# Splitting the weight transfers of the last four expert pairs, not the last two, in a decoder-layer kernel

## The chip, the core and the metric

The kernel runs on one core of a Trainium2 chip. The time is the device time of one execution in microseconds. All arithmetic is in 32-bit floats.

## What is computed

One layer of a decoder for 256 prompt tokens and 64 sample tokens (320 in all, 1024 features): a modulated norm, a mixer (gated MLP heads and a state-space part) with a gated residual, then a modulated norm and a mixture of 32 experts of which each token takes four, a gated residual and a last norm. The mixture is what this text is about:

```
logits = x @ w_router + b_router
top_v, top_i = top_k(logits, 4);  top_w = softmax(top_v)
for each expert e, on the rows of the tokens that chose it:
    g = minimum(xb @ w_gate[e] + b_gate[e], 7.0)
    u = clip(xb @ w_up[e] + b_up[e], -7.0, 7.0)
    y = (g * sigmoid(1.702 * g) * (u + 1.0)) @ w_down[e] + b_down[e]
out[token] = sum over its 4 experts of top_w * y
```

Each of the three matrices of an expert is 1024 x 1024, so an expert has 12.6 MB of weights and all of them 403 MB. Each is used once.

## The kernel before

The first 260 us or so are the mixer and the router (weights `w_front`). Then the experts are worked off in 16 **pairs**, 0 to 15. A pair's two experts share the 128 columns of the TensorE array, 64 token rows for each (`CAP`), or 96 and 32 in pairs 2 to 5. The gathered rows are the stationary operand and the weights stream past them.

*Transfers.* A pair's weights come in 12 transfers (`PER`), numbered k = 0 to 11, of 2 MB each: k even is for the first expert of the pair and k odd for the second, and each brings four chunks (`CHUNKS`) of 128 input features times 1024 outputs of one matrix. So k = 0 to 3 are `w_gate`, 4 to 7 `w_up`, 8 to 11 `w_down`. They land in a ring of 8 slots (`RING`), 16 MB of on-chip memory; `SLOT` says which slot each takes. In the text the fourth transfer of a pair is k = 3, the eighth is k = 7, and so on.

*SyncE* issues all of them in program order (the functions at L566 to L587). Ahead of each it waits for the semaphore `exp_used`, which TensorE raises when it has finished with the slot that the transfer overwrites. The transfer's landing raises `exp_landed` of its slot by 16.

*TensorE.* `pair` (L1010) does the three products gate, up and down of a pair, and between them the gathering of the next pair's rows, the turning of the activations and the combining of the pair before. A `product` (L962) is two bias matmuls and then two halves, p = 0 and 1, of 32 matmuls each; half p needs two transfers, one for each expert. It waits for both `exp_landed` at its start (L976). ScalarE and VectorE take the results from PSUM when `exp_used` says that the product is done.

*Split transfers.* `FS` is 6, so `SPLIT` = 12 - 6 = 6. In the last two pairs, 14 and 15, the transfers k = 6 to 11 are each issued as two of 1 MB, two chunks each, by `load_split` (L522), in the order: first half of k, first half of k + 1, second half of k, second half of k + 1. The first half raises the slot's `exp_landed`, the second one a semaphore left over from the front part (`split_landed`, L477). In these pairs the product waits in two steps: for the two first halves at its start, and for the two second halves ahead of its third chunk (L984 to L986). `split_count` (L480) gives the count to wait for. SyncE waits once for both slots of k and k + 1 before it issues the four halves.

*Loops.* Two pairs are a **turn** (`UNROLL`). All engines run the turns through `turns` (L212): turns 0, 1 and 2 (pairs 0 to 5) are written out, turns 3 to 6 (pairs 6 to 13) are one loop in the program, whose addresses and counts come from registers, and turn 7 (pairs 14 and 15) is written out. SyncE has a loop of its own (L575) over turns 1 to 6. Pair 15 goes through `last_pair` (L1048), which has another order of the small steps: it combines pair 14 between gate and up, and lets the down product begin on the first half of the activations. Behind it come the output additions, the last norm and the stores.

Of the kernel before, what the change touches and what calls it, by code (L numbers as in the profile page):

```python
# [65 lines left out]
FS = 6  # L66
# [5 lines left out]
UNROLL = 2  # L72
PAIRS = NE // 2
LAST = PAIRS - 1
SPLIT = PER - FS
MORE_PAIRS = -(-MORE // 2)
LW = 2 * MORE_PAIRS


def caps(q):  # L80

    return (WIDE, NARROW) if isinstance(q, int) and q in UNEVEN else (CAP, CAP)
# [90 lines left out]
NF = len(FRONT)  # L173
# [32 lines left out]
def wait(eng, sem, count):  # L206

    if not (isinstance(count, int) and count <= 0):
        eng.wait_ge(sem, count)


def turns(engine_loop, body):  # L212

    even = max(UNEVEN) // UNROLL + 1
    for i in range(even):
        body(i)
    with engine_loop(even, PAIRS // UNROLL - 1) as i:
        body(i)
    body(PAIRS // UNROLL - 1)


def further_pairs(engine, there, begin, body, again):


    with engine.If(there(engine, 0) == 1):
        begin()
        body(0)
        with engine.If(there(engine, 1) == 1):
            with engine.Fori(1, MORE_PAIRS) as i:
                with engine.If(there(engine, i) == 1):  # L230
# [4 lines left out]
def build(nc, d, out):  # L235
    with ExitStack() as ctx:
# [240 lines left out]
        def split_landed(k):  # L477
            return front_landed[k - SPLIT]

        def split_count(q, k):  # L480
            return 16 * (len(range(k - SPLIT, NF, FS)) + q - (PAIRS - UNROLL) + 1)

        def exp_slot(j, k):
            return SLOT[(PER * j + k) % RING]
# [13 lines left out]
        def chosen(eng, q):  # L498

            return [eng.value_load(expert_i[0:1, bass.ds(q * 2 + s, 1)], min_val=0, max_val=NE - 1) for s in range(2)]  # L500
# [5 lines left out]
        def _(sp):  # L506
# [9 lines left out]
            def load_unit(k, e, slot):  # L516
                sp.dma_start(ring[:, slot, :], exp_source(k, e)).then_inc(exp_landed[slot], 16)  # L517
# [4 lines left out]
            def load_split(k, e, slots):  # L522

                w = [exp_source(k + s, e) for s in range(2)]
                for part in range(2):
                    c = slice(part * LOAD // 2, (part + 1) * LOAD // 2)
                    for s in range(2):
                        done = exp_landed[slots[s]] if part == 0 else split_landed(k + s)
                        sp.dma_start(ring[:, slots[s], c], w[s][:, c]).then_inc(done, 16)
# [38 lines left out]
            def sorted_pair(i, j):  # L568
                es = chosen(sp, i * UNROLL + j)
                for k in range(PER):  # L570
                    sp.wait_ge(exp_used, i * (PER * UNROLL) + (PER * j + k - RING + 1))
                    load_unit(k, lambda s: es[s], exp_slot(j, k))

            sorted_pair(0, 1)
            with sp.Fori(1, PAIRS // UNROLL - 1) as i:  # L575
                for j in range(UNROLL):
                    sorted_pair(i, j)
            for j in range(UNROLL):
                q = PAIRS - UNROLL + j
                es = chosen(sp, q)  # L580
                for k in range(PER):
                    if k < SPLIT:
                        sp.wait_ge(exp_used, q * PER + k - RING + 1)
                        load_unit(k, lambda s: es[s], exp_slot(j, k))
                    elif k % 2 == 0:
                        sp.wait_ge(exp_used, q * PER + k + 1 - RING + 1)
                        load_split(k, lambda s: es[s], [exp_slot(j, k + s) for s in range(2)])  # L587
# [30 lines left out]
        def _(pe):  # L618
# [262 lines left out]
            for m in range(KC):  # L881
# [5 lines left out]
                for i in range(KC):  # L887
                    k = (i + 4) % KC
# [55 lines left out]
            def gather(q):  # L944

                wait(pe, sel_ready, q + 1)
                wait(pe, selT_ready, q - 1)
                for k in range(KC):
                    for t in range(NT):
                        last = mm(ps[:, 6 + k // 4, (k % 4) * P:(k % 4 + 1) * P], htok[:, t, k * P:(k + 1) * P],  # L950
                                  moe["sel"][:, t, :], t == 0, t == NT - 1)
                    if isinstance(q, int) and q == 0 and k == KC // 2 - 1:
                        last.then_inc(half_mm, 1)
                last.then_inc(x_mm, 1)

            def turn_act():

                for k in range(KC):
                    last = pe.transpose(ps[:, k // 4, (k % 4) * P:(k % 4 + 1) * P], A[:, k, :], cn("ident"))  # L959
                last.then_inc(a_tr, 1)  # L960

            def product(m, bank, rows, loads, slots, widths=(CAP, CAP), between=None, half_done=None, mid=None, q=None):  # L962
# [9 lines left out]
                for p in range(KC // CHUNKS):  # L972
# [8 lines left out]
                    for at, (kk, half) in enumerate(order):  # L981
                        if mid is not None and (p, kk, half) == (0, CHUNKS - 2, 0):
                            mid()
                        if q is not None and at == CHUNKS and m * PER // 3 + 2 * p >= SPLIT:  # L984
                            for s in range(2):
# [9 lines left out]
            def combine(q):  # L995

                pe.wait_ge(y_ready, q + 1)
                pe.wait_ge(selT_ready, q + 1)
                for m in range(KC):
                    wait(pe, comb_added, q * KC + max(0, m - 2))  # L1000
                    mm(ps[:, (2, 3, 6)[m % 3], 0:T], moe["y"][:, m * P:(m + 1) * P], moe["selT"]).then_inc(comb_mm, 1)

            def turn_sel(q):

                pe.wait_ge(selw_ready, q + 1)
                for t, (t0, r) in enumerate(TILES):
                    last = pe.transpose(ps[:, 7, t0:t0 + r], moe["selw"][0:r, t, :], cn("ident", r, r))  # L1007
                last.then_inc(selT_tr, 1)

            def pair(q, slots, loads, serial=False):  # L1010
                first = isinstance(q, int) and q == 0
                if serial:
                    wait(pe, comb_added, q * KC)
                    gather(q)
                if first:
                    pe.wait_ge(half_copied, 1)
                else:
                    pe.wait_ge(x_ready, q + 1)
                pe.wait_ge(pick_ready, q + 1)
                w = (CAP, CAP) if serial else caps(q)  # L1020
                split = isinstance(q, int) and PAIRS - UNROLL <= q < PAIRS
                product(0, 0, X, loads[0:PER // 3], slots[0:PER // 3], w, (lambda: pe.wait_ge(x_ready, 1)) if first else None)
                if first:
                    turn_table()
                if not first:
                    wait(pe, comb_added, (q - (0 if serial else 1)) * KC)
                if isinstance(q, int) and q == 2:
                    pe.wait_ge(more_read, 1)
                product(1, 2, X, loads[PER // 3:2 * PER // 3], slots[PER // 3:2 * PER // 3], w, sort_table if first else None,
                        q=q if split else None)  # L1030
                if not serial:
                    gather(q + 1)
                pe.wait_ge(act_ready, q + 1)
                turn_act()
                if not serial:
                    pe.wait_ge(x_ready, q + 2)
                if not serial and not first:
                    combine(q - 1)
                turn_sel(q)
                pe.wait_ge(actT_ready, q + 1)  # L1040
                wait(pe, y_ready, q)
                later_middle = None
                if isinstance(q, int) and q == 1:
                    later_middle = further_blocks
                product(2, 4, A, loads[2 * PER // 3:PER], slots[2 * PER // 3:PER], w, later_middle,
                        q=q if split else None)
# [48 lines left out]
            def turn_table():  # L1095

                pe.wait_ge(perm_ready, 1)
                mm(ps[:, 5, P:P + NE], cn("eidx", NE), perm[0:NE, :])
                mm(ps[0:NE, 5, 0:1], perm[0:NE, :], count[0:NE, :])
                pe.wait_ge(table_ready, 1)  # L1100
                for t, (t0, n) in enumerate(TILES):
                    last = pe.transpose(ps[0:2 * NE, 4, t0:t0 + n], table[0:n, :, t], cn("ident", n, n))
                last.then_inc(tableT_mm, 1)
# [26 lines left out]
            def pe_turn(i):  # L1130
                for j in range(UNROLL):
# [4 lines left out]
                    else:  # L1136
                        pair(i * UNROLL + j, slots, loads)

            turns(pe.Fori, pe_turn)
            final_sums(0)  # L1140
            pe.wait_ge(more_ready, 1)
# [12 lines left out]
        def _(act):  # L1154
# [204 lines left out]
            def last_copies():  # L1359
# [11 lines left out]
                A(moe["y"][:, AW:D], ps[:, 5, :], ACT.Copy).then_inc(y_ready, 1)  # L1371

            turns(act.Fori, act_turn)

            def squares(r):
# [23 lines left out]
        def _(dve):  # L1399
# [492 lines left out]
            def dve_turn(i):  # L1892
                nonlocal start
                for j in range(UNROLL):
# [29 lines left out]
                    if second:  # L1924
                        start = start + 2

            turns(dve.Fori, dve_turn)
            add_last()
            final_norm(0)
# [168 lines left out]
```

## Time and profile before

| | us |
|---|---|
| median of three runs | 1196.75 |
| lowest, highest of them | 1194.54, 1199.53 |
| the profiled execution, its own time | 1195.16 |
| its span, first to last instruction | 1193.2 |
| TensorE busy, matmuls | 1144.8 (96%) |
| VectorE busy | 293.9 (25%) |
| ScalarE busy | 153.4 (13%) |
| expert weights moved by SyncE's queue | 180 transfers of 2 MB, 24 of 1 MB |
| mean granted TensorE clock, share of full | 0.985 |

Times in the profile count from the first instruction of the span. The share of TensorE in its own span says little here, since a loop in which TensorE and the DMA engines are nearly equally fast shows both as busy. What is wanted is who waits for whom, pair by pair, and which wait is the last one that the end depends on. The line L620 is the helper through which every matmul goes, L517 issues a whole transfer and L529 a half.

### The profile page before, as it was taken

What the parts mean: (1) busy time and instruction counts of PE and PEld (TensorE: products, weight loads), DVE (VectorE), ACT (ScalarE), POOL (GpSimd) and SP (SyncE); (2) the same over time, 40 slices, a digit from 0 to 9 for tenths busy, and PEclk for the clock granted to TensorE, in tenths of its full rate; (3) what the DMA queues carried; (4) which work ended last, traced back from release to release, by engine and by line L of the source; (5) the groups of instructions that cost most, each with busy time, mean ns of one, the idle gap of its engine ahead of it and who ended that gap; (6) DMA issues with size and microseconds to landing.
All of it is one profiled execution on the core that took longest, in us unless ns stands there. A gap on an engine that the chain in (4) does not pass through costs nothing.

```text
span 1193.2 us, 15523 instructions
## 1 busy us (share of the span) xinstructions
PE 1144.8 (96%) x6471; PEld 532.9 (45%) x6472; DVE 293.9 (25%) x667; ACT 153.4 (13%) x258; POOL 32.1 (3%) x46
## 2 busy tenths in 40 slices
PE   5999999999999999999999999999999999999995
PEld 2666556554353524243535353434343444434332
DVE  3254422422121213030303031212121212121143
ACT  1442141311000000000101010101010101011002
POOL 1030201000000000000000000000000000000000
PEclk9899999999999999999999999999999999999998
DMA  9574567649999999999999999999999999999992
GB/s 381 226 272 156 221 272 313 263 183 429 417 428 422 428 422 427 426 427 427 425 428 428 427 426 429 429 430 426 429 429 430 427 428 429 430 427 420 429 419 90
DMA packets 38788, 452.67 MB, mean 379 GB/s; under 512 B 4176, under 2 KB 6608, under 8 KB 7632
## 3 DMA queue, kind: packets, MB, share of 16 engines
q1 hardware_dynamic: 37984, 449.31, 89.8%
q0 software_dynamic: 752, 2.60, 0.6%
q8 instruction: 40, 0.66, 0.2%
q14 instruction: 12, 0.10, 0.0%
HBM read 447.99 MB, written 3.91 MB: 379 GB/s over the span
## 4 chain that ended last, share of the span: by engine, by line
PE 76%; DMA 19%; ACT 2%; DVE 1%; issue 1%; SPq 0%; DVEq 0%
PE ps L620 75%; DMA arena<-in_w_exp 18%; ACT arena L1320 1%; DMA arena<-in_w_front 1%; DVE arena L1404 1%; DMA arena<-in_xT 1%; PE ps L1007 0%; SPq L517 0%; PE ps L776 0%; DVE arena L1810 0%; DVE arena L1808 0%; DVE arena L1789 0%; ACT arena L1180 0%; PE ps L797 0%; PE ps L1065 0%
## 5 line engine op out<-in xcount | busy, mean ns | idle before, releaser
L620 PE MATMUL ps<-arena 128*64 128x512 f32 (+10 forms) x6226 | 1115.5, 519 | 37.5 <-DMA arena<-in_w_exp 14.3
L620 PEld LDWEIGHTS ps<-arena 128*64 128x64 f32 (+4 forms) x6226 | 505.4, 147 | 638.4 <-issue 568.4
L1320 ACT ACTIVATE arena<-ps 128x1024 f32<-128x1024 f32 x45 | 44.4, 1021 | 516.4 <-PE ps L620 516.4
L1746 DVE TENSOR_SCALAR arena<-ps 128x1024 f32<-128x1024 f32 x15 | 18.3, 1223 | 266.0 <-PE ps L620 266.0
L1404 DVE TENSOR_TENSOR arena<-arena 128x1024 f32<-128x1024 f32 (+11 forms) x91 | 66.2, 749 | 53.1 <-ACT arena L1328 16.8
L1404 DVE TENSOR_TENSOR arena<-arena,ps 128x320 f32<-128x320 f32 (+2 forms) x116 | 57.0, 494 | 69.2 <-PE ps L620 64.2
L1754 DVE TENSOR_SCALAR arena<-ps 128x1024 f32<-128x1024 f32 x15 | 18.4, 1224 | 183.6 <-PE ps L620 183.6
L1328 ACT ACTIVATE arena<-arena 128x1024 f32<-128x1024 f32 x16 | 16.9, 1057 | 243.8 <-DVE arena L1746 228.3
L1739 DVE COPY arena<-arena 128x64 f32 (+3 forms) x32 | 5.0, 193 | 124.9 <-PE ps L620 124.9
L1404 DVE TENSOR_TENSOR arena<-ps,arena 128x64 f32<-128x64 f32 (+10 forms) x39 | 13.2, 354 | 40.1 <-PE ps L620 35.3
L1732 DVE TENSOR_SCALAR arena<-arena 128x64 f32<-128x64 f32 (+3 forms) x96 | 23.0, 302 | 0.1
L1462 DVE SCALAR_TENSOR_TENSOR arena<-arena 128x344 f32<-128x344 f32 x24 | 13.7, 576 | 26.0 <-ACT arena L1211 25.3
L1755 DVE SCALAR_TENSOR_TENSOR arena<-arena 128x1024 f32<-128x1024 f32 x15 | 18.4, 1225 | 0.5
L1725 DVE TENSOR_SCALAR arena<-arena 128x64 f32<-128x64 f32 (+3 forms) x96 | 17.0, 246 | 1.9 <-issue 1.5
L959 PE MATMUL ps<-arena 128*128 128x128 f32 x120 | 15.6, 272 | 0.0
L1336 ACT ACTIVATE arena<-ps 128x320 f32<-128x320 f32 x16 | 7.0, 438 | 61.2 <-PE ps L1007 61.2
L959 PEld LDWEIGHTS ps<-arena 128*128 128x128 f32 x120 | 13.6, 140 | 0.0
L1654 DVE SCALAR_TENSOR_TENSOR arena<-ps,arena 128x256 f32<-128x256 f32 x8 | 3.9, 484 | 30.0 <-PE ps L620 30.0
L1007 PE MATMUL ps<-arena 128*128 128x128 f32 (+1 forms) x48 | 9.4, 274 | 0.2 <-ACT arena L1320 0.2
L1007 PEld LDWEIGHTS ps<-arena 128*128 128x128 f32 (+1 forms) x48 | 6.6, 139 | 6.3 <-issue 2.7
L1226 ACT ACTIVATE arena<-arena 128x320 f32<-128x320 f32 x8 | 3.8, 470 | 40.3 <-DVE arena L1404 40.3
L2001 POOL TENSOR_TENSOR arena<-arena 128x1024 f32<-128x1024 f32 x4 | 7.8, 1974 | 35.8 <-DVE arena L1404 35.8
(147 smaller groups left out, 176.2 us busy)
## 6 DMA issues: line engine op xcount, KB each, us to landing
arena<-in_w_exp SPq DMA_DIRECT2D x180, 2048.0 KB, 22.0
arena<-in_w_front SPq DMA_DIRECT2D x38, 1024.0 KB, 9.3
arena<-in_w_exp SPq DMA_DIRECT2D x24, 1024.0 KB, 24.0
arena<-in_s0T SPq DMA_DIRECT2D x1, 2048.0 KB, 15.9
out_ssmsT<-arena POOLq DMA_DIRECT2D x4, 512.0 KB, 5.3
arena<-in_xT SPq DMA_DIRECT2D x1, 1280.0 KB, 6.1
out_yT<-arena SPq DMA_DIRECT2D x4, 320.0 KB, 3.3
arena<-in_vec SPq DMA_DIRECT2D x1, 898.0 KB, 18.7
```

The source lines that it names most:

```text
L620: return pe.matmul(o, l, r, start=start, stop=stop, skip_group_check=True)
L959: last = pe.transpose(ps[:, k // 4, (k % 4) * P:(k % 4 + 1) * P], A[:, k, :], cn("ident"))
L1007: last = pe.transpose(ps[:, 7, t0:t0 + r], moe["selw"][0:r, t, :], cn("ident", r, r))
L1320: A(moe[name].rearrange("p (a b) -> p a b", a=2), ps[:, bank:bank + 2, :], ACT.Copy).then_inc(done, 1)
L1328: A(moe["s"], moe["g"], ACT.Sigmoid, scale=ALPHA).then_inc(sig_ready, 1)
L1404: return V.tensor_tensor(o, a, b, op)
L1462: ins = V.scalar_tensor_tensor(c, line[:, m, k:k + CONVN], conv_w[:, k, m:m + 1], c, ALU.mult, ALU.add)
L1725: ins = V.tensor_scalar(moe["sel"][0:r, t, at:at + n], cn("iota", r, n), place_of(s, t, r), None, ALU.is_equal)
L1732: ins = V.tensor_scalar(moe["selw"][0:r, t, at:at + n], cn("iota", r, n), place_of(s, t, r), weight_of(s, t, r), ALU.is_equal, ALU.mult)
L1746: V.tensor_scalar(halves("g"), blocks(0), LIMIT, None, ALU.min).then_inc(g_ready, 1)
L1754: step(V.tensor_scalar(halves("s"), blocks(2), LIMIT, -LIMIT, ALU.min, ALU.max))
L1755: V.scalar_tensor_tensor(g, s, 1.0, g, ALU.add, ALU.mult).then_inc(act_ready, 1)
```

## The change

The split is extended from the last two pairs to the last four, 12 to 15. Since a loop body can't hold both forms, and the count of `split_count` is a constant, turn 6 (pairs 12 and 13) leaves the loops of all engines and is written out like turn 7. The loop of `turns` then runs over turns 3 to 5 and that of SyncE over turns 1 to 5.

```diff
+SPLIT_TURNS = 2
+SPLIT_PAIRS = 4
...
-    with engine_loop(even, PAIRS // UNROLL - 1) as i:
+    with engine_loop(even, PAIRS // UNROLL - SPLIT_TURNS) as i:
         body(i)
-    body(PAIRS // UNROLL - 1)
+    for i in range(PAIRS // UNROLL - SPLIT_TURNS, PAIRS // UNROLL):
+        body(i)
...
         def split_count(q, k):
-            return 16 * (len(range(k - SPLIT, NF, FS)) + q - (PAIRS - UNROLL) + 1)
+            return 16 * (len(range(k - SPLIT, NF, FS)) + q - (PAIRS - SPLIT_PAIRS) + 1)
...
-            with sp.Fori(1, PAIRS // UNROLL - 1) as i:
+            with sp.Fori(1, PAIRS // UNROLL - SPLIT_TURNS) as i:
                 for j in range(UNROLL):
                     sorted_pair(i, j)
-            for j in range(UNROLL):
-                q = PAIRS - UNROLL + j
+            for q in range(PAIRS - SPLIT_PAIRS, PAIRS):
+                j = q % UNROLL
                 es = chosen(sp, q)
...
-                split = isinstance(q, int) and PAIRS - UNROLL <= q < PAIRS
+                split = isinstance(q, int) and PAIRS - SPLIT_PAIRS <= q < PAIRS
```

All line numbers below L75 move by two or three in the changed kernel: L517 becomes L520, L529 L532 and L620 L623.

On TensorE, the up product of the second pair of a turn (pair 13 in its last round) stands in the loop before as follows. The semaphores are those of the slots for k = 4, 5 and then k = 6, 7; `x15` is a run of equal instructions.

```order
L620 MATMUL ps<-arena 128x512 [waits comb_added]
L620 MATMUL ps<-arena 128x512
L976 REGISTER_ALU
L620 MATMUL ps<-arena 64x512 [waits exp_landed3,exp_landed1]
L620 MATMUL ps<-arena 64x512 x15
L620 MATMUL ps<-arena 64x512 [waits exp_landed5,exp_landed4]
L620 MATMUL ps<-arena 64x512 x15
```

The same product of pair 13 in the changed kernel:

```order
L623 MATMUL ps<-arena 128x512 [waits comb_added]
L623 MATMUL ps<-arena 128x512
L623 MATMUL ps<-arena 64x512 [waits exp_landed3,exp_landed1]
L623 MATMUL ps<-arena 64x512 x15
L623 MATMUL ps<-arena 64x512 [waits exp_landed5,exp_landed4]
L623 MATMUL ps<-arena 64x512 x7
L623 MATMUL ps<-arena 64x512 [waits front_landed1,front_landed0]
L623 MATMUL ps<-arena 64x512 x7
```

The register instruction is gone, and the second half of the product has a wait at its start and another in its middle.

On SyncE, the transfers k = 7 and 8 of a pair in the loop before (`ISA` is the instruction that carries a wait or a register):

```order
L517 ISA [waits exp_used]
L517 DMA arena<-in_w_exp 128x4096
L571 REGISTER_ALU
L517 ISA [waits exp_used]
L517 DMA arena<-in_w_exp 128x4096
```

and k = 6 and 7 of pair 13 in the changed kernel:

```order
L532 ISA [waits exp_used]
L532 DMA arena<-in_w_exp 128x2048
L532 ISA
L532 DMA arena<-in_w_exp 128x2048
L532 ISA
L532 DMA arena<-in_w_exp 128x2048
L532 ISA
L532 DMA arena<-in_w_exp 128x2048
```

Two transfers with a wait ahead of each have become four with one wait ahead of them all.

## Rows read from the trace of the kernel before

**Rows 1.** The page, 40 equal slices: DMA busy in tenths, and rate.

```profile
DMA  9574567649999999999999999999999999999992
GB/s 381 226 272 156 221 272 313 263 183 429 417 428 422 428 422 427 426 427 427 425 428 428 427 426 429 429 430 426 429 429 430 427 428 429 430 427 420 429 419 90
```

**Rows 2.** TensorE's waits, 570 to 1060 us: who for whom, total, times, longest.

```profile
PE ps L620 <- DMA arena<-in_w_exp: 14.1, 8, 2.7
```

**Rows 3.** The chain that ended last, from the loop: start, us, what.

```profile
537.76 22.21 DMA arena<-in_w_exp
...
714.91 22.76 DMA arena<-in_w_exp
...
914.00 14.35 PE ps L620 x80
...
950.07 22.53 DMA arena<-in_w_exp
...
972.73 12.66 PE ps L620 x80
...
1007.21 24.11 DMA arena<-in_w_exp
...
1044.13 1.03 ACT arena L1320
...
1100.62 1.03 ACT arena L1320
```

**Rows 4.** Timeline of TensorE, pairs 12 and 13: start, us, what, idle before.

```profile
972.73 12.64 PE L620 MATMUL ps<-arena 128*64 128x512 f32 x80 [0.33 <-DMA arena<-in_w_exp]
...
1031.45 12.64 PE L620 MATMUL ps<-arena 128*64 128x512 f32 x80 [2.01 <-DMA arena<-in_w_exp]
```

**Rows 5.** The chain that ended last, pair 15.

```profile
1129.71 0.10 issue
...
1142.15 15.01 PE ps L620 x68
...
1163.74 12.82 PE ps L620 x56
```

**Rows 6.** SyncE's issues (start, us) and their time to landing; last, over 1060:1150.

```profile
1058.96 0.33 SPq L517 DMA_DIRECT2D arena<-in_w_exp  x1
...
arena<-in_w_exp SPq DMA_DIRECT2D x1, 2048.0 KB, 21.3
...
1082.61 2.00 SPq L529 DMA_DIRECT2D arena<-in_w_exp  x1
...
arena<-in_w_exp SPq DMA_DIRECT2D x1, 1024.0 KB, 27.5
...
1095.71 0.33 SPq L517 DMA_DIRECT2D arena<-in_w_exp  x1
...
arena<-in_w_exp SPq DMA_DIRECT2D x1, 2048.0 KB, 34.0
...
1139.57 6.10 SPq L529 DMA_DIRECT2D arena<-in_w_exp  x1
...
arena<-in_w_exp SPq DMA_DIRECT2D x1, 1024.0 KB, 29.7
...
DMA to landing us min/median/max: 17.4/24.2/34.0
```

**Rows 7.** DMA queues, packets and MB: 302.2:579.6, 579.6:698.5, 711:1080 (all), 1080:1172.

```profile
q8 instruction: 16, 0.26, 0.4%
...
q8 instruction: 5, 0.08, 0.3%
...
q1 hardware_dynamic: 10943, 158.06, 100.6%
...
q8 instruction: 4, 0.07, 0.3%
```

**Rows 8.** Busy times of two stretches of one pair each; PEclk is third from last.

```profile
816.00:874.70 58.70, 56.45 (x281) 24.41 (x279) 11.59 (x26) 4.45 (x5) 0.00 (x0) 1.00 1.01 428
874.70:933.40 58.70, 56.44 (x273) 24.09 (x272) 10.47 (x24) 4.02 (x4) 0.00 (x0) 0.97 1.01 429
```

## The prediction

> **What bounds the kernel now.** Start with the page's forty slices [rows 1]. From the twelfth slice to the last but one the DMA engines are busy in nine tenths or more and carry a nearly constant 425 to 430 GB/s. TensorE is busy too, so the slices alone don't say which of the two sets the pace. The list of TensorE's waits does [rows 2]: between 570 and 1060 us it waited eight times for an expert transfer, 14.1 us in all, and almost for nothing else. So in the loop the weights are late, and TensorE catches up and stops.
>
> The chain of waits gives the rhythm [rows 3]. It has one transfer in each pair, always the eighth of the twelve (it ends the wait in front of a group of 80 matmuls). A start plus its time is a landing: 537.76 + 22.21 = 559.97, 714.91 + 22.76 = 737.67, 950.07 + 22.53 = 972.60, 1007.21 + 24.11 = 1031.32. The last two are 58.72 us apart, which is 4.89 us for each of twelve transfers. TensorE needs less: the two marks of ScalarE, 1044.13 and 1100.62, are one pair apart with no late transfer between them, and that is 56.49 us. So it gains some 2.2 us on the DMA in each pair and gives it back in front of the eighth transfer. The timeline shows the last two of these stalls, 0.33 us in pair 12 and 2.01 us in pair 13 [rows 4]. Both are in the part that the change now splits.
>
> Then look where the end is set. In pair 15, the last one, the chain has 0.10 us of idle time and goes on at 1129.81 us [rows 5]. The transfer issued at 1095.71 took 34.0 us, so it landed at 1129.7 [rows 6]. That is the fourth transfer of pair 15, a whole one before and after the change. TensorE reached it 0.1 us too early. Everything after it (12.82 us with 56 matmuls from 1163.74, then the output chain) follows without a wait for a transfer. The very last half transfer lands at 1139.57 + 29.7 = 1169.3 [rows 6]; it is needed after 32 of those 56 matmuls, at 0.22 us each (15.01 us for 68), so at 1170.7, with 1.4 us to spare.
>
> **The change part by part.**
>
> *The stalls of pairs 12 and 13.* With the first halves of transfers 7 and 8 landing half-way through the old interval, TensorE starts without stopping: 0.33 + 2.01 = 2.34 us of idle time go from there. But what is late next is the fourth and sixth transfer of pairs 14 and 15, still whole. The DMA never pauses, so being earlier on TensorE doesn't make it earlier: slots come free up to 2.3 us sooner while each transfer already spends 17 to 34 us between issue and landing [rows 6], most of it queued. The fourth transfer of pair 15 can't land before its turn. TensorE was there 0.1 us early; now it is 2.4 us early and waits. Gain at the end: 0.
>
> *The price of halves.* Twelve whole transfers of 2 MB become 24 of 1 MB. Pair 14 has both kinds [rows 6]: its sixth whole transfer lands at 1058.96 + 21.3 = 1080.3, its last half at 1082.61 + 27.5 = 1110.1, so twelve halves take 29.8 us. Six whole ones take 6 x 4.893 = 29.4 us at the loop's rhythm. The cost is 0.4 to 0.5 us for six; with two more pairs, 0.8 to 1.0. A second count with more reach: from 1031.32 to 1169.3 there are 28 transfers' worth (four of pair 13, twelve each of 14 and 15), 137.0 us; they took 138.0. The excess, 0.9 to 1.0 us, belongs to twelve split transfers and to whatever code fetch took in that stretch. All of it comes before pair 15's fourth transfer, because the change splits pairs 12 and 13. It is paid in full: **+0.9 us**.
>
> *The written-out turn.* Pairs 12 and 13 leave the loop. In the loop from 711 to 1080 us no instruction transfer appears; in 579.6 to 698.5, when the loop's code is first read, there are five of 16 KB, and from 1080 to 1172, the written-out last turn, four [rows 7]. So the turn that is written out adds about five. What do they cost? The upper bound: from 559.97 to 737.67 the DMA needed 177.70 us for three pairs, and 3 x 58.72 is 176.16, an excess of 1.5 us with no halves in it. The lower bound: the count of the last paragraph holds four fetches and leaves nothing for them once the halves are paid. The last turn's code is the same as the added turn's, so I take that row: **0**, and keep 1.5 for the range. On TensorE itself a fetch stall of up to 2.3 us would lie under the idle time that the halves free.
>
> *SyncE.* Six further instructions a pair are issued, 0.33 us each, and a half's pair is issued only when the second slot is free. SyncE also gets stuck in an issue when many are outstanding: 2.00 and 6.10 us [rows 6]. Behind it stand only later weight loads, and even the quickest of these transfers landed 17.4 us after its issue, of which its own data are 2.5 to 4.9 us. Cost 0. The added waits on TensorE hold back its own matmuls alone; ScalarE and VectorE need the product's end, which isn't later for them.
>
> The sum is 0 + 0.9 + 0 + 0 = +0.9 us. The profiled execution took 1195.16 us, 2.0 more than its span of 1193.2, and becomes 1196.1. The median of the three runs, 1196.75, is 1.6 above the profiled one; the same 0.9 on it gives **1197.7**.
>
> A rule speaks against splitting. The Trainium skill (DMA: Bandwidth & Descriptors, under Two cost components) gives each DMA a fixed part of about 2.0 us beside its bytes. If twelve more transfers each held the queue for that, the time would be some 24 us more. The row of pair 14 disagrees for a full queue: 0.04 us for each further transfer, so here the fixed part lies beside the transfer in front.
>
> **The rivals.**
>
> *TensorE keeps its 2.3 us* (faster). It needs pair 15's fourth transfer to land 2.4 us before 1129.7. For it: nothing after that transfer waits for DMA, so a gain would pass through until the last half's 1.4 us are used up; that caps it at about 1.4 to 2.3. Against it: the even landings leave no pause to recover. Time 1196.75 - 2.3 = 1194.4. Chance 0.05, and still within 0.5%.
>
> *Code fetches hold up the queue.* The upper bound of above, 1.5 us on top: 1199.2. For it is the excess of the loop's first turn, against it the last turn. Chance 0.15.
>
> *The half clock.* TensorE's new wait in pairs 14 and 15 is 2.4 + 0.9 = 3.3 us in all. After one stall of about 2 us (at 914.00) the same group of 80 matmuls took 14.35 instead of 12.66 us [rows 3], 1.69 us more, and the granted clock of that stretch is 0.97 and not 1.00 [rows 8]: for a part of it 1.2 and not 2.4 GHz. In the loop the next stall swallowed that; behind pair 15's fourth transfer nothing would. Time 1197.7 + 1.7 = 1199.4. It decides if that last stall is long; I expect 1 to 2 us of it there. Chance 0.10.
>
> *Slower by over 0.5%.* Each 16 KB fetch occupies one of the 16 DMA engines for about 1.1 us (0.4% of 16 x 277.4 us, over 16 fetches, [rows 7]). A transfer has landed only when all engines are through. If all five fetches fell on the engine that is behind anyway, the queue would lose 5 x 1.1 = 5.5 us before pair 15: 1196.75 + 0.9 + 5.5 = 1203.2. It decides at five full ones; the worst stretch of the trace lost 1.5 us. Chance 0.04.
>
> **How the numbers follow.** The forecast has 0.66. About 0.5% (6 us) is what a measurement of this kernel can tell from no change; forecast and the first three rivals all lie inside, so 0.93 for no change, 0.02 for faster (no mechanism reaches 6 us; only a run's own spread), 0.05 for slower. The range: downwards the lowest of the runs before plus 0.9 is 1195.4, upwards the two middle rivals at 1199.4 plus 1.8 for a median that lies off by what the runs before differ (1194.54 to 1199.53). That makes 1195.0 to 1201.2.
>
> **What the changed profile would show.** No stall in front of the eighth transfer of pairs 12 and 13. New stalls in front of whole transfers of pairs 14 and 15, together about 3 us, one of them at the fourth transfer of pair 15, near 1130.7. The last half landing near 1170.2 instead of 1169.3. Four to six instruction transfers between 960 and 1080 where there were none. I am wrong if pair 15's fourth transfer lands before 1129.7, if the DMA has pauses in the last four pairs, or if the half clock falls behind that transfer.

## The result and the profile after

| | before | after |
|---|---|---|
| median of 20 runs each, us | 1196.14 | 1199.47 |
| lowest, highest | 1194.18, 1200.52 | 1196.71, 1203.87 |
| ratio after / before, 95% interval | | 1.0025 (1.0015 to 1.0034) |
| profiled execution's span, us | 1193.2 | 1201.2 |

The changed kernel is slower by 0.25% by the ratio (3.0 us) and by 3.3 us of median. That is inside the range and inside the half per cent that was called no change, and on the side that was forecast. But it is more than three times the 0.9 us of the sum, so the sum has terms of the wrong size.

The profiled execution after is the second longest of its twenty. Part of its 8.0 us over the first profile was there ahead of the change: the eighth transfer of pair 11, the last one before the two programs part, landed 3.90 us later. This is scatter of the front part, as far as the traces tell: over all fourteen of them pair 0's last transfer landed between 281.9 us (e1) and 287.6 us (e6), late also in e4, which changes nothing ahead of pair 14. But the second trace of after is late here too (917.36 us, against 912.88 and 914.87 in the later ones of before), so whether any of the timed difference arises ahead of the change is not shown. Everything below is counted **from that landing**. The chain of waits of the changed kernel shows it in its first row, 893.60 + 24.16 = 917.76 us (before: 889.74 + 24.12 = 913.86, read from its chain in the same way as [rows 3]):

```profile
893.60 24.16 DMA arena<-in_w_exp
...
1001.89 24.02 DMA arena<-in_w_exp
...
1026.05 19.52 PE ps L623 x112
...
1060.42 26.25 DMA arena<-in_w_exp
...
1086.80 21.22 PE ps L623 x112
...
1114.12 34.60 PE ps L623 x152
...
1170.87 12.82 PE ps L623 x56
```

Start, us, what. Compare it with [rows 3, 5]. The transfers in the chain are no longer the eighth of each pair but the sixth, whole ones: 1001.89 + 24.02 = 1025.9 in pair 13 and 1060.42 + 26.25 = 1086.7 in pair 14. The same group of 112 matmuls behind them took 19.52 us in pair 13 and 21.22 in pair 14, where the granted clock fell from 2.4 to 1.2 GHz for a part of it (a **half clock** below). And from 1114.12 on TensorE ran through pair 15's fourth transfer with no idle time, where [rows 5] had its 0.10 us.

The timeline of TensorE gives the new stalls (last column: idle before, and what ended it):

```profile
1026.05 19.51 PE L623 MATMUL ps<-arena 128*64 128x512 f32 x112 [1.64 <-DMA arena<-in_w_exp]
...
1077.01 8.14 PE L623 MATMUL ps<-arena 128*64 128x512 f32 x36 [2.32 <-DMA arena<-in_w_exp]
1086.80 5.78 PE L623 MATMUL ps<-arena 128*64 128x512 f32 x18 [1.65 <-DMA arena<-in_w_exp]
```

None is in front of the eighth transfer of pair 12 or 13 [rows 4]; they moved to the sixth of pair 13, the fourth of pair 14 and the sixth of pair 14. TensorE's waits for expert weights went up, not down, against the 14.1 us of [rows 2] (570 to 1180 us here; before has 0.10 us more behind 1060). They scatter too: over the same stretch the later traces of before have 14.4 and 14.5 us, and the second of after 15.1.

```profile
PE ps L623 <- DMA arena<-in_w_exp: 17.7, 10, 2.7
```

Next the busy times by stretch, one for each of the pairs 12 to 15 by the landing of their last transfers; TensorE's clock is third from last, the rate last:

```profile
937.30:996.50 59.20, 58.96 (x293) 24.98 (x293) 11.53 (x26) 4.45 (x5) 0.00 (x0) 1.00 1.01 425
996.50:1057.30 60.80, 58.81 (x291) 26.02 (x289) 11.40 (x26) 4.45 (x5) 0.00 (x0) 1.00 1.01 424
1057.30:1116.40 59.10, 54.89 (x265) 24.68 (x263) 11.41 (x26) 4.45 (x5) 0.00 (x0) 0.97 1.01 424
1116.40:1175.50 59.10, 58.26 (x265) 20.77 (x263) 14.94 (x32) 3.71 (x5) 0.00 (x0) 1.00 0.93 389
```

Three pairs take 59.1 or 59.2 us, as a split pair should. Pair 13 took 60.8, 1.6 more. In pair 14 the granted clock is 0.97, the half clock of above. Lastly the issues of pair 15's fourth transfer and of the very last half, with their times to landing, as in [rows 6], and the instruction transfers of 715 to 960, 960 to 1080 and 1080 to 1176 us, as in [rows 7]:

```profile
1103.10 0.33 SPq L520 DMA_DIRECT2D arena<-in_w_exp  x1
...
arena<-in_w_exp SPq DMA_DIRECT2D x1, 2048.0 KB, 32.9
...
1148.84 1.97 SPq L532 DMA_DIRECT2D arena<-in_w_exp  x1
...
arena<-in_w_exp SPq DMA_DIRECT2D x1, 1024.0 KB, 26.7
...
q1 hardware_dynamic: 7206, 104.94, 100.6%
...
q8 instruction: 4, 0.07, 0.2%
...
q8 instruction: 4, 0.07, 0.3%
```

The fourth transfer of pair 15 landed at 1136.0 and the last half at 1175.5. Counted from pair 11's eighth landing, the first is 218.3 us (before: 1129.7 - 913.9 = 215.8), the last 257.8 (before 255.4). There are four instruction transfers of 16 KB more.

### The profile page after: what moved, and what is told of

It is laid out like the page before. It is cut to its first block, busy times and chain, and to the rows that moved or that the text cites. A ratio compares the mean times of both kernels' runs of the same rounds, so it can differ in the third digit from the quotient of the medians.

```text
span 1201.2 us, 15451 instructions
## 1 busy us (share of the span) xinstructions
PE 1149.2 (96%) x6471; PEld 537.0 (45%) x6472; DVE 293.8 (24%) x667; ACT 153.5 (13%) x258; POOL 32.1 (3%) x46
## 4 chain that ended last, share of the span: by engine, by line
PE 76%; DMA 19%; ACT 2%; DVE 2%; issue 1%; SPq 0%; DVEq 0%
PE ps L623 75%; DMA arena<-in_w_exp 18%; ACT arena L1323 1%; DMA arena<-in_w_front 1%; DVE arena L1407 1%; DMA arena<-in_xT 0%; PE ps L1010 0%; SPq L520 0%; DVE arena L1813 0%; PE ps L779 0%; DVE arena L1811 0%; DVE arena L1792 0%; PE ps L800 0%; ACT arena L1183 0%; PE ps L1068 0%
## 5 line engine op out<-in xcount | busy, mean ns | idle before, releaser
L623 PE MATMUL ps<-arena 128*64 128x512 f32 (+10 forms) x6226 | 1119.7, 520 | 40.9 <-DMA arena<-in_w_exp 18.4
L623 PEld LDWEIGHTS ps<-arena 128*64 128x64 f32 (+4 forms) x6226 | 509.4, 147 | 641.6 <-issue 572.6
L1742 DVE COPY arena<-arena 128x64 f32<-128x64 f32 (+3 forms) x32 | 4.9, 193 | 124.6 <-PE ps L623 124.6
```

The source lines that it names most:

```text
L623: return pe.matmul(o, l, r, start=start, stop=stop, skip_group_check=True)
```

## The experiments

All traces are read in one way. **A** is the time from pair 11's eighth landing to that of pair 15's fourth transfer: the DMA's part up to the place where the prediction pinned the end. **B** goes from there to the last 56 matmuls (1163.74 in [rows 5]): TensorE's part. **C** is the rest, to the end of the span. The ratio is that of interleaved runs on one chip, against the kernel before. A, B and C alone always name these stretches; a theory is called theory A, B or C.

| kernel | A | B | C | ratio (95%) |
|---|---|---|---|---|
| before, first trace | 215.81 | 34.07 | 29.43 | |
| before, second and third trace | 216.15, 216.76 | 34.07, 34.06 | 29.24, 29.69 | |
| after, first and second trace | 218.26, 218.22 | 34.85, 34.07 | 30.35, 30.49 | 1.0025 (1.0015 to 1.0034) |
| e1, turn written out, split as before | 217.42 | 35.46 | 29.66 | 1.0020 (1.0004 to 1.0035) |
| e2, pairs 6 to 15 split, loops as before | 217.26 | 34.69 | 29.65 | 1.0029 (1.0011 to 1.0046) |
| e3, after, halves from the third transfer on | 218.77 | * | * | 1.0007 (0.9993 to 1.0022) |
| e4, pair 15 split only | 215.91 | 35.93 | 30.22 | 1.0017 (1.0003 to 1.0031) |
| e5, after, TensorE kept busy | 218.40 | 34.73 | 30.05 | 1.0043 (1.0027 to 1.0058) |
| e6, after, TensorE alone written out | 218.22 | 34.07 | 29.04 | 1.0025 (1.0011 to 1.0040) |
| e7, two more turns written out | 217.43 | 34.45 | 29.30 | 1.0042 (1.0026 to 1.0058) |
| e8, before, TensorE kept busy in the loop | 216.49 | 34.06 | 29.34 | 1.0013 (1.0000 to 1.0026) |
| e9, six halves fewer than before | 216.00 | 34.06 | 30.47 | 0.9998 (0.9986 to 1.0011) |

(* e3 stops for the very last half, inside the 56 matmuls; B and C together are 63.03, against 63.3 to 63.8 in the three traces of before.)

One column needs no statistics. B is 34.06 or 34.07 us in seven traces of five kernels. It is the fixed work behind pair 15's fourth transfer, and a trace that shows it had TensorE waiting for that transfer. Where B is larger, TensorE came late.

**Theories.** Theory A: the loss is the halves' price, the code fetch's price in the transfer queue and a half clock behind a stall. Theory B: code is free, the halves cost more than counted. Theory C (for the clock alone): it falls by chance, not with stalls.

### e1: the code without the halves

```diff
-SPLIT_PAIRS = 4
+SPLIT_PAIRS = 2
...
-            for q in range(PAIRS - SPLIT_PAIRS, PAIRS):
+            for q in range(PAIRS - SPLIT_TURNS * UNROLL, PAIRS):
                 j = q % UNROLL
+                whole = SPLIT if q >= PAIRS - SPLIT_PAIRS else PER
...
-                    if k < SPLIT:
+                    if k < whole:
```

> The turn of pairs 12 and 13 is written out as in the changed kernel, but only pairs 14 and 15 are split, as before. Theory A (the loss of the changed kernel is 0.9 us of halves, 1 to 1.5 us of code fetch in the transfer queue, and about 1 us of half clock): five more instruction transfers between 960 and 1080 us, the stalls in front of the eighth transfer of pairs 12 and 13 stay, the DMA needs 0 to 1.5 us longer from pair 11's eighth transfer to the last half (255.4 us before), and the time is 0.5 to 1.5 us above the kernel before. Theory B (the code is free and the halves cost more than I counted): same time as before within 0.3 us.

Slower by 0.20%, 2.4 us, with nothing split that wasn't before. Theory B falls. A is 1.2 us above the mean of before's three traces (216.24), and the instruction transfers of 960 to 1080 us are there, where the kernel before has none from 711 to 1080 [rows 7]; here five, the last of them at 1076.7 us for the turn behind:

```profile
q8 instruction: 5, 0.08, 0.3%
```

The rest shows in TensorE's timeline, pair 13. The stall that was 2.01 us in [rows 4] is 3.59, since a late transfer stood in front of it (the seventh of the pair landed at 1026.8 us, 6.2 us behind the sixth and not 4.9; a fetch of 16 KB had begun at 1024.1), and the 80 matmuls behind the stall took 14.34 us and not 12.64, a half clock:

```profile
1031.80 14.34 PE L624 MATMUL ps<-arena 128*64 128x512 f32 x80 [3.59 <-DMA arena<-in_w_exp]
```

B is 35.46: TensorE reached pair 15 1.4 us too late to meet its transfer. Both stretches are over what I expected, 0.5 to 1.5 us.

### e7: twice the code

```diff
-SPLIT_TURNS = 2
+SPLIT_TURNS = 3
```

on top of e1.

> Pairs 10 to 13 are written out, pairs 14 and 15 alone are split. Twice the added code of the kernel that has only the turn of pairs 12 and 13 written out, with the splits of before. Theory A: some ten more instruction transfers than before, and twice the excess, 2.6 to 3.2 us, between pair 9's eighth transfer and the last half; the time 3 to 4 us above the kernel before. If the excess was chance and not the code, it stays at 0 to 1.5 us.

From pair 9's eighth landing (772.22 + 24.11 in its chain of waits) to the last half 375.96 us, against 372.84, 373.80 and 373.75 in the three traces of before and 374.48 in e1: 2.5 us over before's mean, where e1 has 1.0. The step is repeated with the second turn: nine fetches of 16 KB stand between 816 and 1080 us, where before has none. The time is 0.42% higher (5.0 us, from six runs), more than the 3 to 4 us expected and more than the 2.5 us of its trace; where the rest comes from stays open, though the interval's lower end, 3.1 us, lies in the expectation.

With this the fetches can be counted over all traces, from pair 9's last landing to the very last one, less 58.75 us for each of six pairs and 0.08 us for each split transfer (that figure is e2's). With only the last turn written out the excess is -0.19, 0.77 and 0.72 us in the three traces of before, and 0.67, 0.87, 1.27 and 0.68 in e2, e4, e8 and e9: mean 0.7. With two turns out it is 1.30 and 1.20 (after) and 1.44, 1.39, 1.42 and 1.30 (e1, e3, e5, e6): mean 1.3. With three it is 2.91, in the one trace there is. The first trace of the kernel before was the lowest of all fourteen.

That the fetches themselves hold the queue up can be read landing by landing. Between 740 and 1175 us a whole transfer lands 4.89 us behind the one before it and a half 2.48 (the middle values over all traces). In the fourteen traces 27 landings of expert weights came more than 0.2 us later than that, the latest by 1.5 us (at 1054.8 us in the first trace of after, behind a fetch begun at 1051.6). In front of every one of the 27 a fetch of 16 KB had begun, 2 to 7 us earlier. There were 86 such fetches, so most of them cost less than can be told for one landing.

### e2: the halves without the code

```diff
+            def split_pair(i, j):
+                es = chosen(sp, i * UNROLL + j)
+                for k in range(PER):
+                    if k < SPLIT:
+                        sp.wait_ge(exp_used, i * (PER * UNROLL) + (PER * j + k - RING + 1))
+                        load_unit(k, lambda s: es[s], exp_slot(j, k))
+                    elif k % 2 == 0:
+                        sp.wait_ge(exp_used, i * (PER * UNROLL) + (PER * j + k + 1 - RING + 1))
+                        load_split(k, lambda s: es[s], [exp_slot(j, k + s) for s in range(2)])
...
-                split = isinstance(q, int) and PAIRS - UNROLL <= q < PAIRS
+                split = not serial and (not isinstance(q, int) or q >= SPLIT_FROM)
```

with SyncE's loop over turns 3 to 6 calling `split_pair` and `SPLIT_FROM = 6`.

> Pairs 6 to 15 are split, eight more than before, but pairs 6 to 13 stay in the loops, so no code is added on TensorE, VectorE or ScalarE. Theory A: each split pair takes the DMA 0.45 us longer, 59.2 instead of 58.7 us; the stalls in front of the eighth transfers go and others of the same sum stand in front of the fourth or sixth; the time is 8 x 0.45 = 3.6 us above the kernel before, up to 1.7 us more where a half clock falls into pair 14 or 15. Theory B: more than 1 us for each pair, over 8 us in all. If splitting more pairs could gain at all, the time would fall by up to 2.3 us; no theory of mine says so.

0.29%, 3.5 us, for eight more pairs: as theory A has it. In the loop, where no fetch disturbs, the six pairs from 698.1 to 1053.5 us (by their last landings) took 59.23 us each on average, 0.48 above 58.75 and so 0.08 for each split transfer. And no pair in the loop gained from its halves. The stalls of pair 11, for one, are in front of its fourth and sixth transfer, 2.44 us together in place of 2.02 in front of the eighth (the stall that ends at 914.00 in [rows 3]):

```profile
895.55 8.14 PE L627 MATMUL ps<-arena 128*64 128x512 f32 x36 [0.79 <-DMA arena<-in_w_exp]
905.35 7.07 PE L627 MATMUL ps<-arena 128*64 128x512 f32 x24 [1.65 <-DMA arena<-in_w_exp]
```

### e3: take the whole transfers away

```diff
+EARLY = 2
+def whole(q):
+    return EARLY if q >= PAIRS - UNROLL else SPLIT
...
-                    if k < SPLIT:
+                    if k < whole(q):
```

with the same bound in `product`, and four semaphores of the front part reused for the second halves.

> The changed kernel, and in pairs 14 and 15 the transfers k = 2 to 5 are split too, so that only k = 0 and 1 are whole there. Theory A (the whole fourth and sixth transfers of pairs 14 and 15 hold TensorE): TensorE keeps the 2.3 us that it gains in pairs 12 and 13, doesn't wait in front of the fourth transfer of pair 15, and meets the DMA only at the very last half, which lands 0.6 us later for eight more halves. Time 1.5 to 2.5 us below the changed kernel, 0 to 1.7 above the kernel before. Rival: if those transfers hold nothing, the time is that of the changed kernel plus 0.6 us.

The time is 0.18% (2.2 us) under the changed kernel's ratio, as expected, and no different from before within its interval. The two intervals overlap a little, from 1.0015 to 1.0022, so the trace has to carry the reading. In pair 14 it has stalls of 0.57 and 1.32 us in place of 2.32 and 1.65. TensorE doesn't stop at pair 15's fourth transfer; it stops at the very last half, which is as far as it can be ahead:

```profile
1168.47 7.09 PE L632 MATMUL ps<-arena 128*64 128x512 f32 x32
1175.80 8.83 PE L632 MATMUL ps<-arena 128*64 128x512 f32 x40 [0.24 <-DMA arena<-in_w_exp]
```

So the whole transfers of pairs 14 and 15 were the pin. But with the pin away the DMA's own end comes next, by the prediction only 1.4 us behind, and the 20 more split transfers (1.6 us at 0.08 each) and the code have spent more than that.

### e4: one split pair fewer

```diff
+SPLIT_PAIRS = 1
...
-                split = isinstance(q, int) and PAIRS - UNROLL <= q < PAIRS
+                split = isinstance(q, int) and PAIRS - SPLIT_PAIRS <= q < PAIRS
```

on the kernel before, and the same bound on SyncE.

> The kernel before with pair 14 whole, so one split pair. Theory A: a stall of about 2.2 us comes back in front of the eighth transfer of pair 14, the DMA lands everything after it 0.45 us earlier, TensorE passes the fourth transfer of pair 15 without waiting, 2.1 us later than before. Time 1.8 to 2.1 us above the kernel before: the second split pair is the last that brings anything. Rival: if splitting gains nothing anywhere, 0.4 us below.

0.17%, 2.0 us slower, as expected. The stall is back in pair 14, and B is 35.93, 1.9 us too late for pair 15's transfer:

```profile
1093.05 3.22 PE L622 MATMUL ps<-arena 128*64 128x512 f32 x14 [2.02 <-DMA arena<-in_w_exp]
```

Split pairs pay up to the point where TensorE meets a whole transfer that the DMA can't bring sooner. The second pair reaches it.

### e6: whose code it is

```diff
-def turns(engine_loop, body):
+def turns(engine_loop, body, out=1):
...
-            turns(pe.Fori, pe_turn)
+            turns(pe.Fori, pe_turn, SPLIT_TURNS)
```

> The changed kernel, but VectorE and ScalarE keep pairs 12 and 13 in their loops; TensorE and SyncE have them written out. If the fetches that hold up the transfer queue are TensorE's own, which has most of the code, the excess of 1.3 to 1.5 us in pair 13's transfers stays and the time is that of the changed kernel within 0.5 us. If they are those of VectorE or ScalarE, that excess goes and the time falls by 1.4 us.

The ratio is the changed kernel's, 1.0025, and A is the same 218.22. So the fetches that hold up the queue are not those of VectorE and ScalarE, which added nothing that shows. SyncE's turn is written out here as well as TensorE's, and no run parts the two; that it is TensorE's code is argued from its size, some 1,170 matmul and weight-load records in the turn against 120 instructions of SyncE. In its trace the half clock fell in pair 13, early enough: two later stalls took it up, and B is 34.07. The chain of waits, transfer of pair 15 and what follows:

```profile
1101.65 34.64 DMA arena<-in_w_exp
1136.29 0.14 issue
1136.43 11.78 PE ps L623 x48
```

### e5 and e8: the clock

```diff
+WARM = {(13, 1, 0): 3, (14, 0, 1): 4, (14, 1, 0): 3, (15, 0, 1): 2}
...
+                    if (pair_n, m, p) in WARM:
+                        pe.wait_ge(selT_ready, pair_n)
+                        keep_warm(7, WARM[pair_n, m, p])
```

> The changed kernel with matmuls of ones into a free bank of PSUM in front of the whole transfers that TensorE waits for: three (about 0.4 us each) ahead of the sixth transfer of pairs 13 and 14, four ahead of the fourth of pair 14, two ahead of the fourth of pair 15. They fill waiting time and change nothing else. Theory A (part of the loss is a half clock behind a stall in pairs 13 and 14, seen at 1086.9 us in the changed kernel's trace): no half clock between 1020 and 1180 us, 0.5 to 1.5 us below the changed kernel's median. Theory C (the half clock comes by chance and not with stalls, or is absorbed in front of the fourth transfer of pair 15): no change against the changed kernel.

The clock did as theory A says: from 1020 to 1180 us it is granted in full (the changed kernel has 0.99 over the same stretch).

```profile
1020.00:1180.00 160.00, 157.90 (x759) 67.34 (x755) 35.14 (x70) 12.20 (x15) 0.00 (x0) 1.00 0.95 399
```

But the time rose to 1.0043. The fill was too long: with 0.43 us a matmul, the seven of pair 14 outlasted the two waits that they were meant to fill, and that pair has no stall left. Even so TensorE was at pair 15's fourth transfer 0.28 us before it landed (1134.83 against 1135.11 us); the two matmuls put in there ran until 1135.89, and they are the 0.66 us by which B, 34.73, is above 34.07. The trace shows no more than that: A, B and C together are as long as in the changed kernel's first trace, so most of the 2.2 us of rise over its ratio is unexplained. As a measure of what the half clock costs this run decides nothing.

```diff
+                    if warm is not None and (m, p) == (1, 1):
+                        wait(pe, selT_ready, warm)
+                        keep_warm(7, 4)
```

on the kernel before, in the loop's pairs only.

> The kernel before with four matmuls of ones (1.7 us) in the loop, ahead of the seventh and eighth transfer, where TensorE stops for 2.0 us in each pair. The wait is filled, nothing else changes. Theory A: the half clocks behind these stalls go; those of pairs 6 to 12 were absorbed by the next stall, only one behind pair 13's stall reached the end. So the median falls by 0 to 1 us, and the slower of the runs most. If stalls have nothing to do with the clock, no change; if the fill is too long for some pairs, up to 1 us more.

TensorE's waits for weights between 570 and 1180 us fell from 14 us to 1.8, and the clock stayed full:

```profile
PE ps L620 <- DMA arena<-in_w_exp: 1.8, 3, 0.8
...
600.00:1180.00 580.00, 574.62 (x2803) 251.29 (x2800) 118.69 (x258) 45.64 (x55) 0.00 (x0) 1.00 0.99 419
```

The time didn't fall; its interval, 1.0000 to 1.0026, leaves no room for a gain. So taking the half clocks out of the loop brings nothing. That they cost nothing there is read from B, 34.06 with them and without; the time alone can't say it, since the fill may cost something of its own. And theory C falls. Over all fourteen traces there are 32 half clocks between 600 and 1180 us. Each began within 1.3 us of the end of a stall of 1.6 us or more, of which there were 78. None came without one, and e8, which has no such stall there, has none. Behind the other 46 of these stalls the clock stayed full; what decides between them is not shown.

### The two kernels again, and e9

> The kernel before once more, for a second trace. In the first one the DMA lost nothing to the four fetches of the last turn; in four other kernels with the same last turn it lost 0.7 to 1.3 us. If that is chance from one execution to the next, this trace shows something between 0 and 1.3 us from pair 9's last landing to the very last, above 353.5 us for its whole and split transfers.

> A third trace of the kernel before, for the same reading as the second.

> The changed kernel once more, for a second trace. Theory A: 352.5 us for whole transfers, 1.9 for 24 split ones, and 1.3 to 1.5 for eight fetches, so 355.7 us from pair 9's last landing to the very last, as in its first trace (355.72); TensorE stops in front of whole transfers of pairs 13, 14 or 15 and not in front of split ones.

From pair 9's last landing to the last one before took 353.27, 354.23 and 354.18 us, after 355.72 and 355.62: the expectations hold. In after's second trace too the clock fell behind the stall at pair 14's sixth transfer, but TensorE was early enough to wait 0.16 us for pair 15's fourth. It cost nothing there: B is 34.07. A half clock just behind pair 11's last stall is in this trace too (the granted clock is 0.63 from 917.40 to 922.00 us, third from last below), and not in the first one of after. It is also in the first trace of before [rows 3, 8] and not in the second, where the stalls of pairs 12 and 13 are 2.04 us each and not 0.33 and 2.01:

```profile
917.40:922.00 4.60, 4.51 (x14) 1.77 (x16) 0.00 (x0) 0.00 (x0) 0.00 (x0) 0.63 1.05 449
```

```profile
971.76 12.64 PE L620 MATMUL ps<-arena 128*64 128x512 f32 x80 [2.04 <-DMA arena<-in_w_exp]
...
1030.51 4.94 PE L620 MATMUL ps<-arena 128*64 128x512 f32 x22 [2.04 <-DMA arena<-in_w_exp]
```

The two stalls of after's second trace, as told above:

```profile
1085.22 21.21 PE L623 MATMUL ps<-arena 128*64 128x512 f32 x112 [1.65 <-DMA arena<-in_w_exp]
...
1135.72 4.51 PE L623 MATMUL ps<-arena 128*64 128x512 f32 x20 [0.16 <-DMA arena<-in_w_exp]
```

The way forward that the runs leave is fewer halves, not more. Tried last on the kernel before:

```diff
+def split_at(q, k):
+    return (q == LAST - 1 and k in (6, 7)) or (q == LAST and k >= 8)
```

> The kernel before with halves only where a row shows that they spare a stall: k = 6 and 7 in pair 14, k = 8 to 11 in pair 15. Six transfers are split and not twelve. Theory A: the DMA needs 6 x 0.08 = 0.5 us less for the last two pairs, 0.3 of it ahead of pair 15's fourth transfer; TensorE waited 0.1 us there, so the time falls by 0.1 us where the fetches cost nothing and by up to 0.3 us where they cost 0.7 us or more. Below what five rounds can tell, and shown by the trace alone. If TensorE stops for more than 0.3 us in front of one of the transfers made whole, the time rises by that.

0.9998 (0.9986 to 1.0011): no difference that can be measured, and in the trace no stall for weights in pairs 14 and 15 but 0.22 us at pair 15's fourth transfer. Six of before's twelve split transfers do nothing that can be measured.

## Why the prediction was right, and where its sum was not

**What bounds the kernel: right.** DMA in the loop, and the end pinned to the landing of pair 15's fourth transfer. B at 34.06 or 34.07 in seven traces shows it, and e3 and e4 show it from both sides. In the first trace of after TensorE came late and the pin didn't hold.

**The gain is zero: right; where the time is waited away: wrong.** "TensorE was there 0.1 us early; now it is 2.4 us early and waits." It was 0.16 us early in one trace of after and late in the other. The two stalls went and came back as others, but ahead of that transfer: the first of them already in pair 13, and the longest at the fourth and sixth of pair 14. Of the 3.3 us foreseen the second trace has 3.2 (0.29 + 1.12 + 1.65 + 0.16) and the first 5.7 (0.11 + 1.64 + 2.32 + 1.65). The 2.5 us between them are the 1.7 that the second trace had lost to the half clock behind pair 11's stall, and the 0.8 by which TensorE was late in the first. The trace that the prediction read, with its 2.34 us of stalls, had that half clock too; in before's second trace, which has none there, they are 4.1 us.

**The price of halves: right.** +0.9 us predicted. e2 gives 0.08 us a transfer, 0.96 for twelve. Only the figure beside it, "0.04 us for each further transfer", is half of what the same rows give: splitting six transfers makes six more, and 0.4 to 0.5 us over six is 0.07 to 0.08 each.

**The written-out turn: mis-sized.** The step that failed is "The last turn's code is the same as the added turn's, so I take that row: 0". The row was one execution, and the lowest of seven with that turn. A rose by 2.00 us in the mean of the traces (218.24 against 216.24); without the halves 1.04 are left. e1 and e7 show that it is the code and grows with it, the late landings under e7 that it is the fetches, and e6 that it isn't VectorE's or ScalarE's. Both bounds, 0 and 1.5, held; the value between them was chosen by one sample of something that scatters by over 1 us.

**The half clock: right in kind, underweighted.** It was given 0.10 and was to fall behind pair 15's fourth transfer. It fell behind pair 14's sixth in both traces of the changed kernel, and there it is partly taken up by the wait in front of pair 15's fourth. Its cost at the end was 0.78 us in one trace (B 34.85) and nothing in the other.

**How much of it was luck.** The verdict of no change came true with a sum of 0.9 us against 3.0 measured. The measured time is nearer to the two rivals "Code fetches hold up the queue" and "The half clock", at 0.15 and 0.10, than to the forecast, and both happened, the second in part. It held because these rivals, too, lay within half a per cent, and that was said beforehand.

**What stays open.** A and B together make 2.4 us in the mean (2.00 and 0.39). C is 30.4 us after and 29.5 before. About half of that 1.0 us is the last pair of matmuls, which took 1.39 and 1.34 us in the traces of after and 0.82, 0.82 and 1.07 in those of before. e4, e5 and e9 have a C above 30 too, one with more code than before and two without, so it may be scatter; no run was aimed at it.

## What to carry to other kernels

Where a DMA queue and an engine run neck and neck, as here, finer transfers help only up to the first coarse one that the queue can't bring sooner; find it by the landing that the last fixed stretch hangs on, and stop splitting there. Price a written-out loop turn by its code: in this full transfer queue the fetches were not free. And take a cost that scatters from execution to execution from more than one trace, or from all kernels that share the code.

## What the runs showed of the hardware

- The instruction fetches of a written-out turn (about four of 16 KB) hold the saturated transfer queue up by 0.7 us in the mean, in lumps of up to 1.5 us and sometimes not at all, though each keeps one of 16 engines busy for 0.9 to 1.1 us only. All 27 landings that came over 0.2 us late in the fourteen traces have such a fetch in front of them. The Trainium skill (Runtime: NRT & Kernel Launch, Instruction fetch mechanics) calls the crossing of such a block mostly hidden and names full unrolling as what kernels prefer. On the fetching engine the traces agree: in none of the fourteen does TensorE stop for more than 0.08 us between 700 and 1182 us without another engine or a landing as the releaser. But behind it, in a queue that bounds the kernel, e1's 0.20% says otherwise.
- Halving a 2 MB transfer in a full queue costs 0.08 us (e2: 59.23 us a pair with six of them split, 58.75 with none).
- All 32 half clocks in the steady part came behind one of 78 TensorE stalls of 1.6 us or more. Each takes about 1.7 us from the matmuls behind it (14.35 and 12.66 us for the same 80 in [rows 3]). Filling the stalls with matmuls removed them (e8), and was worth nothing where the next stall would have taken them up.
